# Three unread tiles of 32 bytes ahead of the coefficients, of split x and of the mixed heads, in a layer of float32 matmuls split in three

## The chip, the cores and the metric

The kernel runs on one core of a Trainium2 chip. The metric is the device time in microseconds of one execution. Before the change the median of three runs is 1747.68 us (1747.27 to 1749.12).

## What is computed

One decoder layer for 256 tokens of width 2048, in float32. Cut to what matters:

```python
h = x @ w_in + b_in                       # 2048 -> 5120 columns, in five parts
A = silu(layer_norm(causal_conv31(a_val * sigmoid(a_gate))))
Bm = sc_b * causal_conv3(sc_c * sc_h)
x1 = layer_norm(alpha * x + concat(A, Bm) @ w_out + b_out)
q = x1 @ w_q                              # 8 heads, two halves of 128
s = q . sub_keys                          # top 16 of 128, twice; top 16 of the 256 sums
experts, g = best 16 of 16384, softmax    # for every token and head
act = gelu(x1 . peer_u[experts])
f = sum over heads, k of act * g * peer_v[experts]
x2 = layer_norm(alpha * x1 + f)
```

## The kernel before

**Stages.** The kernel computes the experts densely. After the input projection (to about 235 us of the profile) comes the output projection (235 to 330), then the queries with the routing, then the products of x1 with all 16384 rows of peer_u (to about 1184), and the last projection from the 128 tiles of gated activations onto peer_v (1184 to 1735). Half of the last projection for the second block of 128 tokens is not done densely: for columns 0 to 1023 of that block POOL gathers, pick by pick, 128 rows from a copy of peer_v in DRAM (rows, row_late, line 582) and single coefficients (sp_coef, line 588), and DVE adds row times coefficient (line 1312).

**Split operands.** Every float32 product is made from three matmuls in fp32r: high by high, high by low, low by high. Weights stream from DRAM in units of 512 KB, which SP loads into raw (4 buffers) and, in the last projection, also into raw_late (3 more; RING is 7). ACT writes the high part w_hi (line 627), DVE the low part w_lo (line 843), each with SPLIT = 4 buffers; PE multiplies; each stage waits for the one ahead by semaphore, and SP loads a buffer again when DVE is done with it. ACT runs four units ahead of PE, DVE three.

**Which operand is stationary.** A matmul call names the output, the stationary operand, the moving operand. In the input projection, the queries and the products with peer_u the weights are stationary (128 columns) and split x (xt_hi, xt_lo, 256 columns) moves: lines 1411 to 1413. In the output projection mix_hi and mix_lo are stationary and the weights move, 512 columns: lines 1460 to 1462. In the last projection the coefficients (c_sets, made from hid on ACT line 776 and DVE line 1293) are stationary and the weights move, 512 columns: lines 1587 to 1589. For the last four units of the stream parts_of returns tail_hi and tail_lo in place of w_hi and w_lo. The gate matmuls (line 1553) have oh1 stationary and oh2g moving.

**Order of the last projection.** Four tiles are a group; each group has 8 units: column block 0, 2, 1, 3, two units each. Blocks 0 and 1 take one token block (6 matmuls a unit), blocks 2 and 3 both (12 a unit), 72 matmuls a group. The last four groups are run column block by column block. Coefficient sets c0 and c1 alternate in groups 0 to 28, the sets c2, c3 and c4 serve groups 29 to 31.

**Places in SBUF.** Tiles lie one after another, in the order in which they are named, each from a multiple of 32 bytes; an ExitStack that is closed gives its place back, so that later tiles lie over it. Bytes per partition: raw 16384 and w_hi, w_lo 8 x 4096, the first at a multiple of 64; stats 192, mv 16, rstd and neg_mean 8 each, so that what follows starts 288 bytes on. All tiles from c0 through acc, c2 to c4 and tail have sizes that are multiples of 64, except small ones inside the early set that no large matmul reads (prm, scpad: 32 and 8 bytes over together). hid, the early set, the routing tiles and c2 to c4 with tail lie over one another from the end of xt_lo on.

Of the kernel before, what the change touches and what calls it, by code (L numbers as in the profile page):

```python
# [5 lines left out]
P = 128  # L6
# [160 lines left out]
def build(nc, x_t, x_nat, w_in, w_out, w_q, u_w, v_w, params, sub_keys, b_out, ln1_g, ln1_b, ln2_g, ln2_b, out):  # L167
    f32 = mybir.dt.float32
# [10 lines left out]
    with ctx:  # L179
        def sb(name, shape, dt, where=ctx):  # L180
            return where.enter_context(nc.sbuf_tensor(name, shape, dt))
# [8 lines left out]
        mv = sb("mv", [P, TB, 2], f32)  # L190
        rstd = sb("rstd", [P, TB, 1], f32)
        neg_mean = sb("neg_mean", [P, TB, 1], f32)

        def coefs(name, where):
            return [sb(f"{name}_{part}", [P, GROUP, T], f32r, where) for part in ("hi", "lo")]
# [19 lines left out]
        raw_late = sb("raw_late", [P, RAW_LATE, HALF * P], f32, down1)  # L215
        rows = [sb(f"rows{i}", [P, JCOLS], f32, down1) for i in range(ROWS - 1)] + [row_late]
        down1.close()
        xt_hi = sb("xt_hi", [P, KT, T], f32r)
        xt_lo = sb("xt_lo", [P, KT, T], f32r)

        early = ExitStack()
        mix_hi = sb("mix_hi", [P, KT, T], f32r, early)
        mix_lo = sb("mix_lo", [P, KT, T], f32r, early)
# [1462 lines left out]
```

## Time and profile before

| what | value |
|---|---|
| median of three runs | 1747.68 us (1747.27 to 1749.12) |
| span of the profiled execution | 1745.8 us |
| PE, DVE, ACT, POOL busy | 1713.3, 1407.6, 854.0, 540.4 us |
| granted clock of PE, mean | 0.996 |
| moved by DMA | 504.5 MB, mean 289 GB/s |
| input projection, output projection | to 235 us, to 330 us |
| queries, routing, peer_u | to 1184 us |
| last projection | 1184 to 1735 us |

The span runs from the first to the last instruction of one profiled execution. Its own device time isn't given apart; the median of the runs lies 1.9 us above its span. PE is the tensor engine's matmuls, PEld its weight loads. A matmul's duration includes its way through the array, so that those of neighbours overlap: the distance between two starts says how fast they follow one another. The DMA share is the mean busy share of 16 engines; packets that overlap can bring it over 1.

### The profile page before, as it was taken

The page shows a single profiled execution, that of the slowest core. Times are in us where ns is not written, and L with a number is a line of the kernel's source. Part 1 is how long each engine was busy: PE and PEld are TensorE (multiplying, and loading weights), DVE is VectorE, ACT ScalarE, POOL GpSimd, SP SyncE. Part 2 cuts the span into 40 slices and gives each one's busy share as a digit, 9 for nine tenths or more (in the row PEclk, how much of TensorE's full clock was granted, in tenths as well). Part 3 has the DMA queues.
Part 4 walks back from the last instruction along what each step waited for, and adds up shares of the span by engine and source line. Part 5 has one row for each costly group of instructions (what it writes and reads, how often), then busy time and mean ns, then how long its engine had stood idle before and what let it go on. Part 6 is the DMA issues. An engine that isn't in the chain of part 4 may idle for free.

```text
span 1745.8 us, 31461 instructions
## 1 busy us (share of the span) xinstructions
PE 1713.3 (98%) x11910; PEld 1578.1 (90%) x11910; DVE 1407.6 (81%) x1998; ACT 854.0 (49%) x1084; POOL 540.4 (31%) x342
## 2 busy tenths in 40 slices
PE   8999999899999999999999999999999999999997
PEld 8999987799999999999999999998788777878776
DVE  7999997678967677777777777556899898999997
ACT  5544436344544444444444444445555555555544
POOL 0000000288881000000000000004787777777731
PEclk9999999999999999999999999999999999999999
DMA  7787787777777777777677777899899999999994
GB/s 267 267 276 267 234 260 249 273 237 235 250 249 252 238 236 244 247 235 239 237 241 239 236 244 243 282 355 332 314 400 400 399 401 389 400 399 395 369 398 133
DMA packets 173728, 504.52 MB, mean 289 GB/s; under 512 B 19408, under 2 KB 35920, under 8 KB 172624
## 3 DMA queue, kind: packets, MB, share of 16 engines
q1 hardware_dynamic: 134000, 427.08, 70.0%
q0 software_dynamic: 22528, 67.19, 10.0%
q10 hardware_dynamic: 17120, 9.35, 1.8%
q8 instruction: 29, 0.48, 0.1%
q14 instruction: 51, 0.42, 0.1%
HBM read 490.98 MB, written 79.69 MB: 327 GB/s over the span
## 4 chain that ended last, share of the span: by engine, by line
PE 78%; DMA 6%; DVE 6%; issue 5%; POOL 3%; ACT 1%; DVEq 1%; SPq 0%; POOLq 0%; ACTq 0%
PE psum L1411 18%; PE psum L1413 18%; PE psum L1412 18%; PE psum L1587 6%; PE psum L1589 6%; PE psum L1588 6%; POOL sp_coef L588 2%; DVE w_lo L843 2%; DMA raw<-in_v_w_dram 2%; PE psum L1553 2%; DMA raw_late<-in_v_w_dram 1%; PE psum L1460 1%; PE psum L1462 1%; PE psum L1461 1%; DVE psum L1312 1%
## 5 line engine op out<-in xcount | busy, mean ns | idle before, releaser
L627 ACT ACTIVATE w_hi<-raw 128x1024 fp32r<-128x1024 f32 x547 | 578.9, 1060 | 682.1 <-PE psum L1413 487.1
L1411 PE MATMUL psum<-xt_hi,w_hi 128*128 128x256 f32 x2944 | 827.2, 281 | 5.3 <-DVE xt_lo L857 3.1
L1412 PE MATMUL psum<-xt_lo,w_hi 128*128 128x256 f32 x2944 | 822.6, 279 | 0.0
L1413 PE MATMUL psum<-xt_hi,w_lo 128*128 128x256 f32 x2944 | 822.4, 279 | 0.0
L843 DVE TENSOR_TENSOR w_lo<-raw,w_hi 128x1024 fp32r<-128x1024 f32 x479 | 581.8, 1222 | 221.5 <-ACT w_hi L627 219.7
L1411 PEld LDWEIGHTS psum<-xt_hi,w_hi 128*128 128x128 f32 x2944 | 554.3, 188 | 6.6 <-issue 6.0
L1412 PEld LDWEIGHTS psum<-xt_lo,w_hi 128*128 128x128 f32 x2944 | 554.3, 188 | 0.0
L1413 PEld LDWEIGHTS psum<-xt_hi,w_lo 128*128 128x128 f32 x2944 | 554.1, 188 | 0.0
L582 POOL DMA_INDIRECT rows<-v_rows,sp_idx x96 | 130.9, 1364 | 709.7 <-issue 674.9
L1587 PE MATMUL psum<-w_hi,c_hi 128*128 128x512 f32 x752 | 299.7, 399 | 8.9 <-DVE w_lo L843 8.7
L1589 PE MATMUL psum<-w_hi,c_lo 128*128 128x512 f32 x752 | 298.2, 396 | 0.0
L1588 PE MATMUL psum<-w_lo,c_hi 128*128 128x512 f32 x752 | 297.9, 396 | 0.0
L571 POOL TENSOR_TENSOR w_lo<-raw,w_hi 128x1024 fp32r<-128x1024 f32 x68 | 164.7, 2427 | 364.3 <-ACT w_hi L627 364.2
L588 POOL DMA_INDIRECT sp_coef<-hid_spill,sp_idx x128 | 193.0, 1508 | 55.2 <-issue 45.9
L1587 PEld LDWEIGHTS psum<-w_hi,c_hi 128*128 128x128 f32 x752 | 141.7, 188 | 49.5 <-DVE w_lo L843 15.4
L1589 PEld LDWEIGHTS psum<-w_hi,c_lo 128*128 128x128 f32 x752 | 141.6, 188 | 34.3
L1588 PEld LDWEIGHTS psum<-w_lo,c_hi 128*128 128x128 f32 x752 | 141.7, 188 | 33.3
L627 ACT ACTIVATE w_hi<-raw_late 128x1024 fp32r<-128x1024 f32 x105 | 111.3, 1060 | 103.2 <-PE psum L1589 75.0
L843 DVE TENSOR_TENSOR w_lo<-raw_late,w_hi 128x1024 fp32r<-128x1024 f32 x105 | 126.6, 1221 | 8.4 <-ACT w_hi L627 8.4
L1312 DVE SCALAR_TENSOR_TENSOR psum<-rows,sp_coef,psum 128x1024 f32<-128x1024 f32 x95 | 121.8, 1282 | 3.2 <-DMA rows<-v_rows,sp_idx 2.3
L882 DVE SCALAR_TENSOR_TENSOR cacc<-apad,prm,cacc x232 | 101.3, 480 | 0.0
L1293 DVE TENSOR_TENSOR c_lo<-hid,c_hi 128x1024 fp32r<-128x1024 f32 x32 | 39.2, 1224 | 22.9 <-ACT c_hi L776 22.8
(164 smaller groups left out, 1131.8 us busy)
## 6 DMA issues: line engine op xcount, KB each, us to landing
raw<-in_u_w_dram SPq DMA_DIRECT2D x256, 512.0 KB, 4.2
raw<-in_v_w_dram SPq DMA_DIRECT2D x148, 512.0 KB, 8.7
v_rows<-in_v_w_dram SPq DMA_DIRECT2D x128, 512.0 KB, 5.2
raw_late<-in_v_w_dram SPq DMA_DIRECT2D x108, 512.0 KB, 8.9
raw<-in_w_in_dram SPq DMA_DIRECT2D x80, 512.0 KB, 4.3
raw<-in_w_out_dram SPq DMA_DIRECT2D x32, 512.0 KB, 4.5
raw<-in_w_q_dram SPq DMA_DIRECT2D x32, 512.0 KB, 4.5
hid_spill<-hid ACTq DMA_DIRECT2D x7, 1024.0 KB, 15.4
```

Source lines behind the costliest of these rows:

```text
L571: nc.gpsimd.tensor_tensor(w_lo[s][:, :], raw[:, s, :], w_hi[s][:, :].bitcast(f32), ALU.subtract).then_inc(lo_done[s], SPLIT)
L582: nc.gpsimd.indirect_dma_start(rows[k % ROWS][:, :], None, v_rows, bass.IndirectOffsetOnAxis(sp_idx[:, 1, k:k + 1], 0)).then_inc(rows_in[k ...
L588: nc.gpsimd.indirect_dma_start(sp_coef[:, k:k + 1], None, hid_dram, bass.IndirectOffsetOnAxis(sp_idx[:, 0, k:k + 1], 0)).then_inc(act_in[k ...
L627: nc.scalar.activation(parts_of(slot_u)[0][:, :], raw_of(slot_u), ACT.Copy).then_inc(hi_done, 1)
L843: tt(lo_w[:, :], raw_of(slot_u), hi_w[:, :].bitcast(f32), ALU.subtract).then_inc(lo_done[slot_u % SPLIT], SPLIT)
L1312: i = stt(picked[:, :], rows[k % ROWS][:, :], sp_coef[:, k:k + 1], picked[:, :], ALU.mult, ALU.add)
L1411: mm(dst, hi_w[:, sl], xt_hi[:, kk, :], start=st, stop=False)
L1412: mm(dst, hi_w[:, sl], xt_lo[:, kk, :], start=False, stop=False)
L1413: i = mm(dst, lo_w[:, sl], xt_hi[:, kk, :], start=False, stop=en)
L1587: mm(v_bank(j, b), c1, w1, start=st, stop=False)
L1588: mm(v_bank(j, b), c1, w2, start=False, stop=False)
L1589: i = mm(v_bank(j, b), c2, w1, start=False, stop=en)
```

## The change

Three tiles of 8 float32 (32 bytes a partition) that nothing reads or writes are named: one ahead of the coefficients, one ahead of split x, one ahead of what lies behind split x. No instruction is added, removed or moved. After it, modulo 64 bytes and counted from the split weights, c0, c1, the tiles that lie over them (gates, tables), raw_late and rows are at 0; split x is at 32, as before; mix, hid, the early and routing tiles, c2 to c4 and tail are at 0. Before, all of these were at 32.

```diff
@@ -190,6 +190,7 @@
         rstd = sb("rstd", [P, TB, 1], f32)
         neg_mean = sb("neg_mean", [P, TB, 1], f32)
+        sb("place_pad", [P, 8], f32)
 
         def coefs(name, where):
             return [sb(f"{name}_{part}", [P, GROUP, T], f32r, where) for part in ("hi", "lo")]
@@ -215,11 +216,13 @@
         rows = [sb(f"rows{i}", [P, JCOLS], f32, down1) for i in range(ROWS - 1)] + [row_late]
         down1.close()
+        sb("xt_pad", [P, 8], f32)
         xt_hi = sb("xt_hi", [P, KT, T], f32r)
         xt_lo = sb("xt_lo", [P, KT, T], f32r)
 
 
 
+        sb("early_pad", [P, 8], f32)
         early = ExitStack()
         mix_hi = sb("mix_hi", [P, KT, T], f32r, early)
         mix_lo = sb("mix_lo", [P, KT, T], f32r, early)
```

## Rows read from the trace of the kernel before

**Rows 1.** the page's part 1: engine, busy us, share of the span, instructions

```profile
...
PE 1713.3 (98%) x11910; PEld 1578.1 (90%) x11910; DVE 1407.6 (81%) x1998; ACT 854.0 (49%) x1084; POOL 540.4 (31%) x342
```

**Rows 2.** groups by form: line, operands, shapes, count, busy us, mean ns, idle before

```profile
...
L1411 PE MATMUL psum<-xt_hi,w_hi 128*128 128x256 f32 x2944 | 827.2, 281 | 5.3 <-DVE xt_lo L857 3.1 <-issue 2.3
...
L843 DVE TENSOR_TENSOR w_lo<-raw,w_hi 128x1024 fp32r<-128x1024 f32 x479 | 581.8, 1222 | 221.5 <-ACT w_hi L627 219.7
...
L1587 PE MATMUL psum<-w_hi,c_hi 128*128 128x512 f32 x752 | 299.7, 399 | 8.9 <-DVE w_lo L843 8.7
...
L843 DVE TENSOR_TENSOR w_lo<-raw_late,w_hi 128x1024 fp32r<-128x1024 f32 x105 | 126.6, 1221 | 8.4 <-ACT w_hi L627 8.4
...
L1460 PE MATMUL psum<-w_hi,mix_hi 128*128 128x512 f32 x128 | 51.0, 399 | 1.9 <-DVE mix_lo L997 1.1 <-DVE lnt L1024 0.8
...
L1553 PE MATMUL psum<-oh2g,oh 128*128 128x256 f16 x256 | 34.7, 277 | 0.0
...
L1587 PE MATMUL psum<-tail_hi,c_hi 128*128 128x512 f32 x16 | 6.2, 390 | 0.0
```

**Rows 3.** PE in order of time near the end: start us, us, line, operands

```profile
...
1718.97 0.40 PE L1587 MATMUL psum<-tail_hi,c_hi 128*128 128x512 f32 x1
...
1724.41 0.40 PE L1587 MATMUL psum<-w_hi,c_hi 128*128 128x512 f32 x1
...
1730.02 0.39 PE L1587 MATMUL psum<-tail_hi,c_hi 128*128 128x512 f32 x1
```

**Rows 4.** busy us (count) of PE, PEld, DVE, ACT, POOL; clock, DMA share, GB/s

```profile
...
1719.00:1724.40 5.40, 5.40 (x25) 4.48 (x24) 5.33 (x7) 0.95 (x1) 0.00 (x0) 1.00 0.00 0
1724.40:1730.00 5.60, 5.60 (x25) 4.51 (x24) 5.22 (x12) 2.50 (x6) 1.02 (x1) 1.00 0.00 0
```

**Rows 5.** PE in order of time, output projection

```profile
...
235.87 0.40 PE L1460 MATMUL psum<-w_hi,mix_hi 128*128 128x512 f32 x1
...
237.27 0.40 PE L1460 MATMUL psum<-w_hi,mix_hi 128*128 128x512 f32 x1
```

**Rows 6.** PE in order of time, a 256-column unit

```profile
...
899.78 0.28 PE L1412 MATMUL psum<-xt_lo,w_hi 128*128 128x256 f32 x1
...
900.71 0.28 PE L1411 MATMUL psum<-xt_hi,w_hi 128*128 128x256 f32 x1
```

**Rows 7.** PE in order of time, one batch of gate matmuls

```profile
...
594.35 1.08 PE L1553 MATMUL psum<-oh2g,oh 128*128 128x256 f16 x8
```

**Rows 8.** transfers of 1300 to 1700: GB/s in 40 slices; loads, median us to landing

```profile
...
GB/s 400 400 399 398 398 403 402 399 396 399 403 399 402 398 400 368 384 399 402 399 401 401 402 399 404 387 403 400 402 378 399 393 384 338 343 409 409 408 408 398
...
raw<-in_v_w_dram SPq DMA_DIRECT2D x105, 512.0 KB, 9.2
raw_late<-in_v_w_dram SPq DMA_DIRECT2D x81, 512.0 KB, 9.5
```

**Rows 9.** stretches, columns as in Rows 4

```profile
...
235.00:330.00 95.00, 92.63 (x403) 74.09 (x402) 74.85 (x94) 47.48 (x51) 4.07 (x2) 1.00 0.77 259
1184.00:1260.00 76.00, 74.85 (x319) 59.44 (x319) 56.82 (x51) 42.67 (x42) 47.45 (x37) 1.00 0.90 323
1260.00:1640.00 380.00, 374.42 (x1590) 298.60 (x1589) 356.79 (x317) 208.38 (x201) 293.28 (x202) 1.00 1.02 396
1500.00:1600.00 100.00, 99.46 (x426) 79.50 (x425) 96.62 (x86) 56.09 (x55) 77.04 (x54) 1.00 1.03 398
1640.00:1736.00 96.00, 93.50 (x398) 74.07 (x396) 83.19 (x86) 48.32 (x49) 30.72 (x23) 1.00 0.78 297
```

**Rows 10.** waits of 1260 to 1640: who for whom, us, times, longest

```profile
...
ACT w_hi L627 <- PE psum L1589: 121.7, 108, 2.2
...
ACT w_hi L627 <- DMA raw<-in_v_w_dram: 27.7, 27, 2.4
...
ACT w_hi L627 <- DMA raw_late<-in_v_w_dram: 21.2, 19, 1.8
```

## The prediction

> **What bounds the kernel now.** I read the busy shares first, then the two views that put a price on one matmul, then the one stage in which TensorE is not alone at its limit. PE is busy 98% of the span [rows 1]. So the end is set by how fast PE starts one matmul after another, and for that the duration column is of no use (281 and 399 ns, and they overlap); starts have to be subtracted. Three forms carry the span [rows 2]: 8832 matmuls of 256 columns (lines 1411 to 1413, x2944 each), 2256 + 48 of 512 columns in the last projection (lines 1587 to 1589, x752 and x16 each), and 384 of 512 columns in the output projection (lines 1460 to 1462, x128 each).
>
> Near the end the same three lines alternate between two kinds of operand within 11 us, on an idle DMA [rows 3, 4]. Units whose split weights lie in tail_hi/tail_lo: 24 starts from 1718.97 to 1724.41, 5.44 us, 226.7 ns apart. Units in w_hi/w_lo: 24 starts from 1724.41 to 1730.02, 5.61 us, 233.8 ns apart. The reader is to see that DVE (5.33 of 5.40 us and 5.22 of 5.60 us) is equally busy in both, that nothing is transferred in either, and that the clock is 1.00 in both [rows 4]. The slow spacing is the same 1500 us earlier under traffic: 235.87 to 237.27 us has 6 intervals, 233.3 ns [rows 5], in a stretch with a DMA share of 0.77 [rows 9]. So the 7 ns belong to the operands.
>
> **What distinguishes the operands.** Counting sizes modulo 64: w_hi and w_lo are at 0; stats to neg_mean take 288 bytes, so the coefficients, split x, mix and tail are all at 32. The last projection multiplies c (stationary, 32) by w (moving, 0), slow, or by tail (moving, 32), fast. The output projection is (32, 0), and slow [rows 5]. The 256-column units are (0, 32): 899.78 to 900.71, 8 intervals, 116.3 ns [rows 6], just half of 233. The gate matmuls are (32, 32), also 256 columns: eight of them end 1.08 us after the first starts [rows 7], and each takes 277 ns [rows 2], so seven intervals take 0.80 us, 115 ns: nearer to the fast rate's half (113.4) than to the slow one's (116.9), but no proof by itself. An absolute residue of the moving operand alone doesn't fit: the 256-column units have it at 32, as tail has, and run at the slow rate per column. Equal or unequal fits all. What no row shows is the pair (0, 0), which the change makes.
>
> **Part 1, place_pad:** coefficients c0 and c1 go to 0. **Part 3, early_pad:** mix, c2 to c4 and tail go to 0. **Part 2, xt_pad:** split x stays at 32 against w at 0, so the 8832 matmuls are left as they are: 0. The 48 tail matmuls stay an equal pair: 0. Gates, transposes and scores keep their pairs (both sides move by 32): 0. No instruction, wait or queue is added. Elementwise operands and DMA targets move too: raw against raw_late in the trace is exactly residue 0 against 32, and DVE takes 1222 against 1221 ns [rows 2], the landing 9.2 against 9.5 us [rows 8]; the last could be worth a per cent of the transfers' rate, or nothing; I take 0 and keep -1 to +3 us for it.
>
> **What PE alone would gain.** 2256 x 7.0 ns = 15.8 us in the last projection and 384 x 7.0 = 2.7 us in the output projection, 18.5 us. That is all, if nothing else is late: 1745.8 - 18.5 = 1727.3 us of span; the median of the runs lies 1.9 us above the profiled span, which I add: 1729.2.
>
> **What is late next.** In the output projection PE waited twice, 1.1 us for mix_lo and 0.8 us for the norm of the convolution [rows 2]. These chains don't get faster, so of the 1.3 us won ahead of the second half up to all can come back as wait: between 1.3 and 2.7 us, I take 2.0.
>
> The last projection is where it decides. From 1260 to 1640 us the DMA share is 1.02 at 396 GB/s [rows 9], in slices of 10 us mostly 398 to 403 [rows 8]; ACT waited 49 us of it for landings (27.7 + 21.2) and 122 us for PE [rows 10]; DVE is 93.9% busy (356.8 of 380). What arrives is the unit loads plus the row gathers, and both are paced by PE's units, so a PE that is 3% faster (7.0/233.8) asks for 3% more per us. PE already loses 5.6 us in these 380.
> - 1184 to 1260: DMA share 0.90 [rows 9], 74.9 us of PE x 3% = 2.2 us; DVE is busy 57 of 76 us, the transfers' last tenth is what is left, so I take 1.8.
> - 1260 to 1640: PE would like 374.4 x 3% = 11.2 us. The transfers can give only this: at the rate of the full slices, 400 GB/s, the same bytes (380 x 396) take 376.2 us, 3.8 us less; and the lead of the ring may be eaten up once. A load lands 9.2 to 9.5 us after its issue, one is issued every 2.15 us (105 + 81 in 400 us) [rows 8], so 4.3 of the 7 buffers are in flight and 2.7 are ahead, at most 5.8 us, of which PE can lose some 3.5 before it stops at the bursts. 3.8 + 3.5 = 7.3 us. DVE would need 93.9% / 0.975 = 96% of the time; for that and its queueing behind picks I take 0.4 off: 6.9.
> - 1640 to 1736: 93.5 x 3% = 2.8 us. The mean share there is 0.78 [rows 9], but the slices up to 1700 still read 398 to 409 GB/s [rows 8] and only what follows is free, so I take 1.8.
>
> Sum: 2.0 + 1.8 + 6.9 + 1.8 = 12.5 us. Span 1733.3, time 1735.2 us.
>
> **Rivals.**
> - *The transfers don't matter, PE takes all:* they are kept full only since buffers are free. For it: in 1500 to 1600 PE is 99.46% busy beside a share of 1.03 [rows 9]. Time 1729.2. The Trainium skill, page "DMA: Bandwidth & Descriptors", section "Where 436 GB/s comes from", gives a ceiling of 435 GB/s for the ports; by it 3% more than 400 would have room, and the time would be this one. No slice here goes over 409 [rows 8].
> - *The transfers hold everything while they are full:* the lead is worth nothing and the DVE queue eats the rest. Output 1.3 + early 1.8 + 3.8 less 1 us of DVE queueing + 1.0 at the end = 6.9 us: 1740.8.
> - *The period is 128 bytes, not 64:* by the sizes, c4 and tail, the fast pair, are equal modulo 128 as well, so the trace can't tell. Then c0 and c1 (64 off) gain nothing, and mix and c2 to c4 do: 2.0 us + three groups of 72 less the 48 tail ones, 168 x 7.0 ns = 1.2 us: 1744.5.
> - *No effect:* what makes tail fast is its place or that it is rewritten once, not its residue. Time 1747.7, and with tail's advantage lost 48 x 7 ns = 0.3 us more. Two pages of the Trainium skill speak for it: "TensorE: Matmul & The Clock Gate", in its walk through the matmul's steps, says that PE has two independent SBUF read ports, so that loading the next weights takes nothing from the running matmul; "SBUF — State Buffer", section "SBUF: two separate sides", that PE never waits on anyone. By either the relative place of the two operands could cost nothing; the starts of [rows 3] show 7 ns between two places, which neither explains.
> - *Slower:* the cost is of the two streams meeting in one half of a 64-byte line at offset 0 (only 32 with 32 is seen fast). If (0, 0) is as much worse than (32, 0) as (32, 32) is better, the 2256 + 384 matmuls cost 7.0 ns more each, 18.5 us, and the 48 of the tail 14 ns, 0.7 us: 1766.9. It ends above before as soon as (0, 0) is over 234 ns apart. Against it: nothing in [rows 3 to 7] depends on the sign of the difference: (0, 32) and (32, 0) cost the same per column.
>
> **How the numbers follow.** The forecast (equal pair fast, transfers take a third of it) 0.45; PE takes all 0.17; transfers hold it 0.18; period 128 0.06; no effect 0.09; slower 0.05. A measurement of this kernel can tell about 0.2%, 3.5 us, from no change: period 128, at -3.2, falls to "same" or just beside it, and I give it half to each. Faster 0.45 + 0.17 + 0.18 + 0.03 = 0.83, same 0.12, slower 0.05. The range goes from all for PE with the transfers' bonus down to 1728.5, and up to 1744.5, with period 128 at its edge; left out are no effect and slower, 0.14.
>
> **What would show it.** Starts of lines 1587 to 1589 and 1460 to 1462 some 226.7 ns apart where nothing waits, 116.3 ns still in the 256-column units; up to 235 us the trace unchanged to 0.5 us; the last projection begins 2 us earlier; from 1260 on a share of 1.03 with few lower stretches, ACT's wait for landings up from 49 us to 70 or more, PE's idle time in the last projection up from about 9 to 14 us. If starts stay at 233.8, the pair is not the cause; if only lines with c2 to c4 and mix speed up, the period is 128; if starts are fast and PE's idle time doesn't grow, the first rival holds.

## The result

The changed kernel takes 1776.6 us (median of 4 runs, 1774.7 to 1779.2) against 1747.5 us before in the same comparison: ratio 1.0162, 95% interval 1.0142 to 1.0181. It is 29 us slower where 12.5 us less was forecast; 1735.2 and the range of 1728.5 to 1744.5 are both missed, on the other side.

The page of the changed kernel, span and busy shares (columns as before):

```profile
span 1772.7 us, 31461 instructions
...
PE 1741.4 (98%) x11910; PEld 1605.7 (91%) x11910; DVE 1407.9 (79%) x1998; ACT 854.6 (48%) x1084; POOL 541.9 (31%) x342
```

PE is busy 98% of the span as before [rows 1], and 28 us longer in all. The groups of PE by form, to be laid beside [rows 2]: lines are three further down, the counts are the same, and the mean of the 256-column matmuls is 284 instead of 281 ns, that of the 512-column ones 397 instead of 399.

```profile
...
L1414 PE MATMUL psum<-xt_hi,w_hi 128*128 128x256 f32 x2944 | 835.3, 284 | 4.2 <-DVE xt_lo L860 2.3 <-issue 1.9
...
L1590 PE MATMUL psum<-w_hi,c_hi 128*128 128x512 f32 x752 | 298.9, 397 | 8.9 <-DVE w_lo L846 8.5
...
L1463 PE MATMUL psum<-w_hi,mix_hi 128*128 128x512 f32 x128 | 50.9, 398 | 1.9 <-DVE mix_lo L1000 1.0 <-DVE lnt L1027 0.9
```

PE in order of time in a 256-column unit (start us, us, line, operands), for [rows 6], and in the last projection:

```profile
...
899.80 0.28 PE L1415 MATMUL psum<-xt_lo,w_hi 128*128 128x256 f32 x1
...
900.76 0.29 PE L1414 MATMUL psum<-xt_hi,w_hi 128*128 128x256 f32 x1
```

```profile
...
1599.81 0.39 PE L1590 MATMUL psum<-w_hi,c_hi 128*128 128x512 f32 x1
...
1601.68 0.39 PE L1592 MATMUL psum<-w_hi,c_lo 128*128 128x512 f32 x1
```

Eight intervals take 0.96 us, 120.0 ns, where [rows 6] have 116.3. In the last projection eight intervals take 1.87 us, 233.8 ns: nothing won. The stretches, to be laid beside [rows 9] (busy us and count of PE, PEld, DVE, ACT, POOL; granted clock, DMA share, GB/s), the last three 28 us later than there:

```profile
...
600.00:1000.00 400.00, 400.00 (x3344) 396.22 (x3343) 284.14 (x375) 183.24 (x308) 0.00 (x0) 1.00 0.72 233
1212.00:1288.00 76.00, 74.22 (x317) 58.94 (x316) 55.95 (x50) 42.33 (x42) 47.57 (x36) 1.00 0.89 321
1288.00:1668.00 380.00, 375.06 (x1598) 298.82 (x1597) 358.19 (x318) 209.35 (x203) 296.11 (x202) 1.00 1.02 397
1668.00:1764.00 96.00, 92.32 (x394) 73.17 (x392) 83.89 (x87) 47.96 (x49) 30.59 (x23) 1.00 0.78 293
```

From 600 to 1000 us PE is never idle and does 3344 matmuls; before it did 3433 in the same 400 us (shown below, beside x_up_64). DMA share, rate and DVE's share in the last projection are those of before.

Taken apart by the starts of the first and the last matmul of each stage: input projection 231.9 us (before 225.7), output projection 92.5 (92.7), queries to peer_u 878.0 (856.0), last projection 550.2 (551.4). The input projection and the third stage are the two with 256-column matmuls. Together they take 28.2 us more, a little over the 26.9 by which the whole span grew. 8832 matmuls at 119.97 instead of 116.66 ns (means of all distances under 140 ns between starts of these lines) are 29.2 us.

### The profile page after: what moved, and what is told of

Its sections match the earlier page's. It is cut to its first block, busy times and chain, and to the rows that moved or that the text cites. A ratio compares the mean times of both kernels' runs of the same rounds, so it can differ in the third digit from the quotient of the medians.

```text
span 1772.7 us, 31461 instructions
## 1 busy us (share of the span) xinstructions
PE 1741.4 (98%) x11910; PEld 1605.7 (91%) x11910; DVE 1407.9 (79%) x1998; ACT 854.6 (48%) x1084; POOL 541.9 (31%) x342
## 4 chain that ended last, share of the span: by engine, by line
PE 84%; DMA 5%; DVE 4%; issue 3%; POOL 1%; ACT 1%; DVEq 0%; SPq 0%; POOLq 0%; ACTq 0%
PE psum L1416 20%; PE psum L1415 20%; PE psum L1414 20%; PE psum L1590 6%; PE psum L1592 6%; PE psum L1591 6%; DVE w_lo L846 2%; DMA raw_late<-in_v_w_dram 2%; PE psum L1556 2%; DMA raw<-in_v_w_dram 1%; PE psum L1463 1%; PE psum L1465 1%; PE psum L1464 1%; DVE psum L1315 1%; DMA rows<-v_rows,sp_idx 1%
## 5 line engine op out<-in xcount | busy, mean ns | idle before, releaser
L1416 PE MATMUL psum<-xt_hi,w_lo 128*128 128x256 f32 x2944 | 832.9, 283 | 0.0
L585 POOL DMA_INDIRECT rows<-v_rows,sp_idx x96 | 142.6, 1485 | 723.9 <-issue 691.6
L591 POOL DMA_INDIRECT sp_coef<-hid_spill,sp_idx x128 | 183.1, 1430 | 55.6 <-issue 46.4
L1590 PEld LDWEIGHTS psum<-w_hi,c_hi 128*128 128x128 f32 x752 | 141.2, 188 | 49.9 <-DVE w_lo L846 15.8
```

Of the source, the lines that this page charges most:

```text
L585: nc.gpsimd.indirect_dma_start(rows[k % ROWS][:, :], None, v_rows, bass.IndirectOffsetOnAxis(sp_idx[:, 1, k:k + 1], 0)).then_inc(rows_in[k ...
L591: nc.gpsimd.indirect_dma_start(sp_coef[:, k:k + 1], None, hid_dram, bass.IndirectOffsetOnAxis(sp_idx[:, 0, k:k + 1], 0)).then_inc(act_in[k ...
L1416: i = mm(dst, lo_w[:, sl], xt_hi[:, kk, :], start=False, stop=en)
L1590: mm(v_bank(j, b), c1, w1, start=st, stop=False)
```

## The experiments

Distances here are those from the start of the stationary operand to the start of the moving one, modulo 256 where nothing else is said. By the sizes (raw starts 1152 bytes into a partition): split x lies 46368 bytes behind w_hi0 in the kernel before, that is 32 modulo 256 (288 modulo 1024), and 96 (352) in the changed one. Weights less coefficients is 224 before; in the changed kernel 192 for c0 and c1, and 128 for mix and c2 to c4. The spacings in the tables are means over the starts in the trace of each run.

**Which tile does it.** Four kernels, one pad each:

```diff
# x_up_64 (x_up_32 and x_up_128 with [P, 8] and [P, 32])
+        sb("xt_pad", [P, 16], f32)
         xt_hi = sb("xt_hi", [P, KT, T], f32r)
# all_up_64
+        sb("first_pad", [P, 16], f32)
         raw = sb("raw", [P, RAW, HALF * P], f32)
```

> One unread tile of 64 bytes ahead of split x and nothing else: split x lies exactly where the changed kernel has it (63968 against 63904 bytes), while c0, c1, raw_late and rows stay where the kernel before has them. If the place of split x against the split weights is what made the 256-column matmuls slower (theory X), their starts are 119.9 to 120.0 ns apart, as after, and the time is 1747.5 + 29 = 1776 us. If it was another tile that moved (theory O: coefficients, gate tiles or raw_late, as operands or as neighbours), the starts stay at 116.7 ns and the time at 1747 us. If only residues modulo 64 count, as I had predicted, also 116.7 ns.

> 32 bytes ahead of split x: equal to the split weights modulo 64, 64 off modulo 128. By the residue modulo 64 with equal pairs fast (my recorded theory) the 256-column starts are 113.4 ns apart: 8832 x 3.3 ns less, 1718 us. By a distance with a period of 128 or more (theory X) it is a new point, between 113 and 120 ns. By theory O 116.7 ns, 1747 us.

> 128 bytes ahead of split x. If what counts has a period of 128 bytes, the 256-column starts are again 116.7 ns apart and the time is 1747 us. If the period is 256 or longer, or it is no period at all, they differ from 116.7 ns by over 0.5 ns.

> 64 bytes ahead of raw, the first tile: every tile lies 64 bytes further, all distances between tiles are as before. If distances between operands count, nothing changes: 116.7 and 233.3 ns, 1747 us. If the absolute place of split x counts (it is again at 63968, as in the changed kernel), the 256-column starts are 120 ns apart and the time is 1776 us.

Measured: x_up_64 1779.1 us, ratio 1.0169 (1.0147 to 1.0191), 119.97 ns; x_up_32 1755.9 us in one run, 117.8 ns; x_up_128 1764.6 us in one run, 118.4 ns; all_up_64 1747.1 us in one run, 116.7 ns. The stretch of 600 to 1000 us, in the order before, x_up_64, all_up_64, where the count of PE is what tells the pace:

```profile
...
600.00:1000.00 400.00, 400.00 (x3433) 396.51 (x3433) 293.00 (x385) 187.34 (x314) 0.00 (x0) 1.00 0.72 239
```

```profile
...
600.00:1000.00 400.00, 400.00 (x3345) 396.29 (x3344) 284.47 (x374) 183.01 (x309) 0.00 (x0) 1.00 0.72 234
```

```profile
...
600.00:1000.00 400.00, 400.00 (x3434) 396.50 (x3433) 292.59 (x384) 187.70 (x316) 0.00 (x0) 1.00 0.75 239
```

Moving split x by the 64 bytes by which the change moves it gives the whole loss. Moving everything by 64 bytes gives nothing, though split x then lies where the changed kernel has it: not a place counts but a distance. The pad ahead of split x also moves what lies behind it (mix, hid, the routing tiles, c2 to c4, tail); c0, c1, raw_late and rows stay where they were, so they have no part in the loss. That it is split x and none of the tiles behind it is shown by all_aligned and x_64_rest_0 further down: they differ, modulo 1024, in the place of split x alone, and their starts are 119.9 and 117.8 ns apart. x_up_32, equal modulo 64, is slower than before and not faster: the residue modulo 64 is not the measure.

**Distances as a whole.** In all_aligned the four small tiles are named last instead of ahead of the coefficients, so that all distances are 0 modulo 1024. In the two runs with steps the four buffers lie 32 bytes apart from each other:

```diff
# all_aligned
-        stats = sb("stats", ...)   # and mv, rstd, neg_mean: moved behind sp_tok
# steps_0_to_96, also
-        w_hi = [sb(f"w_hi{i}", ...) for i in range(SPLIT)]
-        w_lo = [sb(f"w_lo{i}", ...) for i in range(SPLIT)]
+        for i in range(SPLIT):
+            if i:
+                sb(f"slot_pad{i}", [P, 8], f32)
+            w_hi.append(sb(f"w_hi{i}", ...))
+            w_lo.append(sb(f"w_lo{i}", ...))
# steps_128_to_224, also
+        sb("behind_pad", [P, 32], f32)
```

> The 288 bytes of stats, mv, rstd and neg_mean are named last, behind sp_tok, instead of ahead of the coefficients; nothing is added. Every distance between two operands of a large matmul is then a multiple of 1024 bytes, as tail against c4 is in the kernel before (its starts are 226.7 ns apart). Theory X1 (distance 0 is the fast one in every form): 256-column starts 113.4 ns apart, 512-column 226.7 ns; PE alone would gain 8832 x 3.3 + 2640 x 7.0 = 47.6 us, of it the transfers hold back up to 11 in the last projection: 1700 to 1712 us. Theory X2 (distance matters, but 0 is good only where the weights move against coefficients, and other distances are best in the other form): 512-column starts 226.7, 256-column ones at 116.7 to 120 ns. Theory X3 (what made tail fast is not its distance): 512-column starts stay at 233.3 ns and the time is 1747 us or above.

> As all_aligned, but the four buffers of the split weights lie 0, 32, 64 and 96 bytes further (high and low part alike), so that one run holds four distances in each form: split x less weights 96, 64, 32, 0 bytes in buffers 0 to 3 (the last modulo 1024), weights less coefficients and less mix the negatives of these. The time says little; the starts inside a unit, sorted by buffer, are what is read. By the single distances seen so far for the 256-column form (32: 116.7, 64: 117.8, 96: 120.0 ns, measured modulo 256): buffer 2 at 116.7, buffer 1 at 117.8, buffer 0 at 120.0 if the period is 256 or a divisor; if it is longer, other numbers. Buffer 3 by X1 at 113.4 and 226.7 ns.

> As steps_0_to_96, with 128 bytes more behind the split weights: split x less weights 224, 192, 160, 128 bytes in buffers 0 to 3, weights less coefficients the negatives. For 160 the run with 128 bytes ahead of split x showed 118.4 ns: buffer 2 repeats it if the period is 256. If the period is 128, buffers 0 to 3 repeat 96, 64, 32, 0 of the other run.

Measured: all_aligned 1772.4 us, ratio 1.0142 (1.0121 to 1.0164), 256-column starts 119.9 ns apart, 512-column ones 227.2 in the last and 227.0 in the output projection. PE in order of time in its last projection, seven intervals in 1.59 us:

```profile
...
1599.86 0.39 PE L1589 MATMUL psum<-w_hi,c_lo 128*128 128x512 f32 x1
...
1601.45 0.39 PE L1587 MATMUL psum<-w_hi,c_hi 128*128 128x512 f32 x1
```

So tail was fast by its distance, and 0 is the fast distance with 512 moving columns and a bad one with 256 (X2). The runs with steps, one execution each (1766.8 and 1759.9 us), sorted by buffer, for the 256-column form:

| distance of x from weights | 0 | 32 | 64 | 96 | 128 | 160 | 192 | 224 |
|---|---|---|---|---|---|---|---|---|
| ns, stepped buffers | 119.8 | 117.0 | 114.7 | 120.0 | 118.8 | 119.6 | 114.4 | 118.4 |
| ns, all buffers alike | 119.9 | 116.7 | 117.8 | 120.0 | | 118.4 | see below | |

32, 96 and 0 repeat what kernels with all buffers alike showed. 64 does not (114.7 against 117.8 in x_up_32), and 160 does not either (119.6 against 118.4 in x_up_128), which the expectation had put as the sign of a period of 256. Here a mean hides two values: at its one distance x_up_128 ran at 117.3 ns in the queries and the first units of peer_u (340 to 522 us) and at 118.7 ns before and after. So a distance can have more than one spacing, and what the neighbouring buffers do counts; that asked for the next runs.

**Fast distances for both forms, and what holds the last projection.**

```diff
# x_64_rest_0: all_aligned, and (x_192_rest_0: 192 bytes, and 832)
+        sb("xt_pad", [P, 16], f32)
         xt_hi = sb("xt_hi", [P, KT, T], f32r)
...
+        sb("mix_pad", [P, 240], f32, early)     # brings mix back to 0
+        sb("late_pad", [P, 240], f32, down2)    # c2 to c4 and tail too
# aligned_less_dve: all_aligned, and
-    i = stt(picked[:, :], rows[k % ROWS][:, :], sp_coef[:, k:k + 1], picked[:, :], ...)
+    i = stt(picked[:, 0:DCH // 2], rows[k % ROWS][:, 0:DCH // 2], sp_coef[:, k:k + 1], picked[:, 0:DCH // 2], ...)
# aligned_less_dma: all_aligned, and for n % 2 and n >= 24
-    sp.dma_start(raw_of(u), src)
+    sp.dma_start(raw_of(u)[:, 0:3 * DCH // 2], src[:, 0:3 * DCH // 2])
```

> As all_aligned, with split x 64 bytes behind the split weights (modulo 1024) in all units; mix and all coefficient sets stay at 0. Theory P256 (the pattern repeats after 256 bytes): split x at 64 is the same as the 320 of the run with 32 bytes ahead of split x, so 117.8 ns between 256-column starts, 119.9 to 117.8 against all_aligned, 1772 - 19 = 1753 us. Theory P-long (it does not repeat before 512 bytes): buffer 1 of steps_0_to_96 was at 64 and showed 114.65, so 114.7 ns; 8832 x 5.2 = 46 us less than all_aligned, 1726 us, which would be 21 us under the kernel before.

> The same with split x 192 bytes behind. In steps_128_to_224 the buffer at 192 showed 114.4 ns. Theory P-long: 114.4 ns, 1724 us, as good as 64 or better. If a buffer's neighbours in the other run made it fast (theory N: what the three other buffers do counts), both this and x_64_rest_0 come out between 116 and 120 ns, 1740 us or above.

> all_aligned, with each of the 127 later picks added over 256 of its 1024 columns only (the other 768 columns of the second token block's first half get the first pick alone); every transfer is left as it is. all_aligned has 512-column starts 6.3 ns closer than before, 14.2 us, but its last projection takes 549.3 against 551.4 us: PE's stalls there, clock drops among them, rose from 14 to 26 us. Theory T (the transfers' rate holds it): stalls stay over 20 us, the stage at 547 us or more. Theory V (DVE, 94% busy, holds it): stalls fall to 5 us or less, the stage takes 527 to 532 us.

> all_aligned, with every second unit load of the last projection, from the 25th on, cut to three quarters of its columns (the rest of the buffer holds an older unit); DVE, ACT and PE do all they did. The unit loads ask for an eighth less, 31 of 400 GB/s. Theory T: stalls fall to 5 us or less and the stage takes 527 to 532 us. Theory V: stalls stay over 20 us. If both this and aligned_less_dve fall half way, each is late on its own, and their sum decides.

Measured: x_64_rest_0 1757.6 us, ratio 1.0045 (1.0028 to 1.0061), 117.8 ns; x_192_rest_0 1754.1 us, ratio 1.0020 (1.0009 to 1.0030). 114 ns, which the stepped run had shown, came in neither but for one stage. Theory P256 holds: 64 with all buffers alike is as slow as the 320 of x_up_32, so these two are one distance, and 256 is a multiple of the period. In x_192_rest_0 the same operands at the same distance had two spacings, in order of time:

```profile
...
149.75 0.28 PE L1415 MATMUL psum<-xt_lo,w_hi 128*128 128x256 f32 x1
...
150.66 0.28 PE L1414 MATMUL psum<-xt_hi,w_hi 128*128 128x256 f32 x1
```

```profile
...
699.75 0.28 PE L1415 MATMUL psum<-xt_lo,w_hi 128*128 128x256 f32 x1
...
700.69 0.28 PE L1414 MATMUL psum<-xt_hi,w_hi 128*128 128x256 f32 x1
```

Eight intervals in 0.91 us (113.8; the mean up to 230 us is 113.3 with single distances of 113 and 114), then in 0.94 us (117.5; mean 117.8), and no unit lies between, but for the first few of either stretch. So at 192, and by the stepped run at 64, there are two rhythms, and either holds for hundreds of matmuls. The fast one did not shorten this execution: its input projection took 221.5 us where x_192_again (below, the same program) took 227.6, but its output projection took 94.0 instead of 90.7, with 3.1 instead of 1.3 us of waiting for mix_lo and 3.4 us at half the granted clock, and its last projection 555.1 instead of 549.2.

aligned_less_dve leaves out three quarters of the columns that DVE adds for the later picks; aligned_less_dma leaves out a quarter of every second load, an eighth of these bytes. The last projection, by first and last start: all_aligned 549.3 us, aligned_less_dve 547.9 us, aligned_less_dma 542.9 us, against 551.4 before. PE's time above its pace in it (all distances over 260 ns, less 233 ns each) is 14.4 us before, 25.7 in all_aligned, 24.1 less DVE, 19.7 less DMA. The middle of it in all_aligned, aligned_less_dve and aligned_less_dma (columns as above):

```profile
...
1290.00:1670.00 380.00, 368.55 (x1589) 296.67 (x1587) 354.77 (x315) 210.08 (x203) 287.93 (x204) 1.00 1.02 395
```

```profile
...
1290.00:1670.00 380.00, 370.89 (x1602) 299.20 (x1601) 282.55 (x320) 210.79 (x203) 251.25 (x208) 1.00 1.03 399
```

```profile
...
1290.00:1670.00 380.00, 373.41 (x1626) 304.49 (x1625) 362.86 (x324) 212.76 (x206) 308.32 (x207) 1.00 1.00 371
```

all_aligned does 1589 matmuls in 380 us, before 1590 [rows 9], though its starts are 6 ns closer. With 72 of 355 us of DVE's work taken away the share of DMA stays at 1.03 and ACT's wait for landings rises, from 63.5 to 143.1 us; PE does 1602:

```profile
...
ACT w_hi L627 <- DMA raw<-in_v_w_dram: 85.7, 80, 3.3
...
ACT w_hi L627 <- DMA raw_late<-in_v_w_dram: 57.4, 58, 2.7
```

With transfers taken away ACT no longer waits for one in that stretch and PE does 1626, at DVE 95% busy. Less work for DVE gives 1.4 us and leaves 24.1 us of stalls, as theory T had it. Less to transfer gives 6.4 us, not the 17 to 22 that theory T had put (527 to 532 us), and 19.7 us of stalls, just under what V had put. So the transfers bind first. That DVE binds next is argued from its 95% and from PE's waits there, which are all for w_lo; no run relieves both.

**The forecast's own case, and a way to the fast rhythm.**

```diff
# x_32_rest_0: as x_64_rest_0 with 32 bytes ahead of split x (992 ahead of mix and of c2)
# buffers_64_192: x_64_rest_0, and
-        w_hi = [...]; w_lo = [...]
+        for i in (0, 2, 1, 3):
+            if i == 1:
+                sb("slot_pad", [P, 32], f32)
+            w_hi[i] = sb(f"w_hi{i}", ...)
+            w_lo[i] = sb(f"w_lo{i}", ...)
# parts_192_64: x_64_rest_0, and
         w_hi = [...]
+        sb("part_pad", [P, 32], f32)
         w_lo = [...]
```

> As x_64_rest_0 with split x 32 bytes behind the split weights (modulo 1024) and all stationary coefficients and mix at 0: my forecast's own case, the 256-column units left at the pace of before and every 512-column matmul at 226.7 ns. Before has split x at 288 modulo 1024. If the pattern has a period of 256 (theory P256), 288 and 32 are the same and the starts are 116.7 ns apart; if not, another number. With 116.7 ns, the output projection 2.0 us shorter (as in all_aligned) and the last projection between 549 and 553 us, as in all_aligned and x_64_rest_0 (transfers hold it), the time is 1744 to 1748 us. By the sum of my prediction it would be 1735.

> The same program as x_192_rest_0, whose profile had 113.3 ns between 256-column starts up to 230 us and 117.8 ns from 335 us on, at one and the same distance. Theory M (at 192 and 64 bytes two rhythms hold themselves, and which one is caught is set by how the stream starts after a pause): the profile of this other execution shows 113.3 in some stages and 117.8 in others, not in the same ones as before, or the same ones if the start is alike; no value between. If the spacing were a function of distance and stage alone, it repeats 113.3 and 117.8 in the same places.

> Split x 192 bytes behind the split weights in buffers 0 and 2, 64 bytes behind them in buffers 1 and 3 (weights less coefficients -128 and 0). Theory M: in steps_0_to_96 and steps_128_to_224 the buffers at 64 and 192, entered from a buffer at another distance, showed 113.5 to 114.9 ns; if a change of distance at each unit lets the stream catch the fast rhythm, these are 113.3 to 115 ns here too, and the time is 1747 - 8832 x 2 to 3 ns, 1722 to 1730 us, plus at most 3 for the last projection. If the rhythm, once 117.8, holds over a change of 128 bytes, all stay at 117.8: 1757 us.

> Split x 192 bytes behind the high part and 64 bytes behind the low part of the weights, so that the distance changes twice in each group of three matmuls. Theory M with a change that lets the fast rhythm be caught: 113.3 to 115 ns, 1722 to 1730 us. If the slow rhythm holds over the change: 117.8 ns, 1757 us. If a change itself costs: over 117.8 ns.

Measured: x_32_rest_0 1747.6 us over 12 runs (1740.8 to 1750.5), ratio 0.9983 (0.9970 to 0.9997), 116.7 and 227.2 ns, output projection 90.7 us, last projection 551.7 us. x_192_again 1754.2 us, 117.8 ns in every stage: the rhythm of the input projection was another one in this execution of the same program. buffers_64_192 1723.3 us, ratio 0.9855 (0.9831 to 0.9878), 113.4 ns in the input projection and 114.4 later; parts_192_64 1721.3 us, ratio 0.9841 (0.9817 to 0.9864), 113.4 and 113.5 ns. The stretch of 600 to 1000 us of x_64_rest_0, x_192_again and parts_192_64:

```profile
...
600.00:1000.00 400.00, 400.00 (x3401) 396.44 (x3400) 290.66 (x382) 185.65 (x312) 0.00 (x0) 1.00 0.69 237
```

```profile
...
600.00:1000.00 400.00, 400.00 (x3401) 396.44 (x3400) 290.89 (x382) 185.64 (x312) 0.00 (x0) 1.00 0.74 237
```

```profile
...
600.00:1000.00 400.00, 400.00 (x3521) 396.52 (x3521) 300.74 (x395) 192.82 (x325) 0.00 (x0) 1.00 0.76 245
```

3521 matmuls in 400 us against 3401, and 3433 before. A distance that alternates between 64 and 192 by part held spacings of 113 to 115 ns in nearly every unit of the two profiles taken (parts_192_64, and parts_and_256 below). By buffer the fast rhythm was lost in the queries, where nearly all units ran at 117.8 ns, and in one unit in six of peer_u beside the gates. PE in order of time in the queries of buffers_64_192, 12 intervals in 1.41 us, 117.5 ns:

```profile
...
389.76 0.28 PE L1419 MATMUL psum<-xt_lo,w_hi 128*128 128x256 f32 x1
...
391.17 0.28 PE L1419 MATMUL psum<-xt_lo,w_hi 128*128 128x256 f32 x1
```

A distance that stays at either of the two caught the fast rhythm in one of eight stages seen (the input projection and what follows, in x_up_32, x_64_rest_0, x_192_rest_0 and x_192_again). Why a stream falls into it, and what the rhythm is of, the records do not show: in the two stretches of x_192_rest_0 most weight loads start 2 to 5 ns after a matmul in both; they take 187 or 188 ns in the fast one, and in the slow one a third of them 192.

**Where tiles begin that are loaded.** In these two kernels the last projection took only 542.0 and 543.2 us, with 512-column starts 230.5 and 228.9 ns apart, and the rate of the transfers was higher. Their raw_late and rows begin at multiples of 256 bytes of a partition; in all kernels ahead of them at 96, 128, 160, 192 or 224 beyond one.

```diff
# x_32_from_256: x_32_rest_0, and
+        sb("first_pad", [P, 32], f32)
         raw = sb("raw", [P, RAW, HALF * P], f32)
# parts_and_256: parts_192_64 with raw named behind w_lo
```

> x_32_rest_0 with 128 unread bytes ahead of raw, the first tile. All distances between operands stay, so PE's starts stay (116.7 and 227.1 ns). raw, raw_late and the rows now begin at multiples of 256 bytes of a partition (raw began at 1152, 128 beyond one). Theory W (transfers into tiles that begin at multiples of 256 bytes go faster): as in buffers_64_192 and parts_192_64, whose rows and raw_late lay at such multiples, the full slices of the last projection read 412 to 415 GB/s instead of 400 to 403, and the stage gets shorter, 535 to 542 us instead of 551.7, so 1731 to 1738 us. Theory S (those two kernels moved more because their PE stage came at another pace, 229 to 230.5 ns): 400 to 403 GB/s, 1747 us.

> parts_192_64 with raw behind the split weights instead of ahead of them: distances as there (192 and 64 bytes, weights less coefficients -128 and 0), and raw too at a multiple of 256 bytes, not only raw_late and the rows. By theory W the four sevenths of the unit loads that go to raw get faster too: another 1 to 3% of rate in the full slices and 1 to 5 us less in the last projection than the 543.2 of parts_192_64, 1716 to 1720 us. By theory S 1721 us, and 1721 too if only the rows matter.

Measured: x_32_from_256 1739.0 us, ratio 0.9922 (0.9901 to 0.9944), 116.7 and 227.1 ns, last projection 544.7 us; parts_and_256 1717.4 us over 5 runs, ratio 0.9793 (0.9771 to 0.9815), last projection 549.6 us in its profile. The transfers of 360 us of the last projection, x_32_rest_0 and then x_32_from_256, from 80 us after its start (GB/s in 40 slices; loads, median us from issue to landing):

```profile
...
GB/s 398 390 375 403 382 394 360 401 402 398 400 402 399 400 403 399 398 403 401 398 399 390 383 384 393 398 401 402 398 403 398 381 383 379 402 400 401 404 387 398
...
raw<-in_v_w_dram SPq DMA_DIRECT2D x96, 512.0 KB, 8.9
raw_late<-in_v_w_dram SPq DMA_DIRECT2D x71, 512.0 KB, 9.1
```

```profile
...
GB/s 378 401 398 416 343 382 331 418 415 416 416 419 417 416 419 400 395 418 417 415 417 418 418 416 418 417 416 416 418 418 407 375 383 418 418 391 376 378 402 356
...
raw<-in_v_w_dram SPq DMA_DIRECT2D x98, 512.0 KB, 7.5
raw_late<-in_v_w_dram SPq DMA_DIRECT2D x73, 512.0 KB, 7.5
```

Full slices go from 398 to 404 up to 415 to 419 GB/s, and a load lands after 7.5 instead of 8.9 us, with every distance between operands kept. Theory W holds for the rate; the stage, 544.7 us, stayed 3 us above what it had put. The Trainium skill, page "DMA: Bandwidth & Descriptors", section "How a descriptor splits into AXI transactions", says of the transactions that read that they must start at a multiple of 256 bytes, so that a descriptor that starts elsewhere pays for the bytes from the boundary below it. It does not say so of the place that is written, which is what moved here. These rows agree in direction, with 4% for packets of 4096 bytes. By an estimate from that page, a packet that starts 128 bytes beyond a boundary takes 17 transactions in place of 16, 6% more, or 132 pieces of 32 bytes in place of 128, 3% more. raw seems to count beside raw_late and rows: with the latter two at multiples (parts_192_64) the full slices read mostly 409 to 415 and a load into raw landed after 8.7 us, with all three (parts_and_256) they read 415 to 420, and the load took 7.5. But the last projection of parts_and_256 took 6.4 us longer than that of parts_192_64 and not less, as was expected, in one execution each; the cause is open.

## Why the prediction was wrong

**The measure was wrong (What distinguishes the operands).** That the 7 ns belong to the operands was right, and all_aligned showed that they come from the distance: 227 ns at 0 in both 512-column stages. The failed step is "Equal or unequal fits all", counted modulo 64. The facts under it were tail at 0 (fast), the other 512-column matmuls at 224 and the 256-column ones at 32 (slow), and the gates at 0 (called no proof). They fit any period of 64 or more. I named 128 as a rival and stopped there. The period is 256: 64 and 320 bytes both give 117.8 ns and 32 and 288 both 116.7, while 32 and 160, 128 apart, differ.

**Part 2 was costed at nothing (xt_pad).** "Split x stays at 32 against w at 0, so the 8832 matmuls are left as they are: 0" is the step that turned the sign. It stays at 32 modulo 64, but goes from 32 to 96 modulo 256, and that costs 8832 x 3.3 = 29 us: x_up_64 has the whole loss alone. It was the term with by far the largest count, and it deserved bounds from both sides, since of distances other than 0 only 32 and 224 had been seen.

**Parts 1 and 3 bring nothing to PE.** 15.8 and 2.7 us were forecast; c0 and c1 land at 192, mix and c2 to c4 at 128, and the starts stay at 233.2 and 232.9 ns. So -18.5 us by PE alone became -0.3. The rival of a period of 128 had mix and c2 to c4 faster; they are not.

**The term for the last projection was too large even with the spacing given.** x_32_rest_0 is the case that the forecast meant. Its output projection is 2.0 us shorter, as put; its last projection 551.7 us against 551.4, where 10.5 us less was forecast. In all it came out 1.9 us under the kernel before of the same comparison (1749.5), where the forecast had 12.5 and the rival that the transfers hold everything 6.9. That rival had the mechanism, but its price for the last projection, 5.6 us, was too high as well: neither the lead of the ring (3.5 us of the forecast) nor the slices not quite full (3.8 us of both) were to be had. PE's waits in that stage rose from 8.7 to 17.8 us. In its middle the rate was 395 GB/s with slices down to 360, not fuller than before, and the granted clock was at half for 6.8 us and again for 3.4 us, against 3.4 us before. That each longer stall of PE also holds up the loads that wait for its buffers would explain it, but no run tests that.

**The targets of transfers were read modulo 64 too (the term of -1 to +3 us).** "Exactly residue 0 against 32" compared raw with raw_late, which lie 128 and 160 bytes beyond a multiple of 256, and the change took raw_late to 192. None of these is at a multiple; with raw, raw_late and rows at multiples the last projection is 7 us shorter (x_32_from_256 against x_32_rest_0).

**The rivals of the other side.** "Slower" was put as (0, 0) modulo 64 being bad for 512 columns, 1766.9. The change made that pair in all 512-column matmuls but those of tail's units, and the starts stayed at 233 ns; in all_aligned, where it is also 0 modulo 256, they are 227 ns apart. So the 0.05 given to "slower" met the sign by another cause, the distance of split x, which that rival left alone. "No effect" is refuted as a cause of tail's speed by all_aligned. The rules cited from the Trainium skill ("TensorE: Matmul & The Clock Gate" on two independent read ports, "SBUF — State Buffer", section "SBUF: two separate sides", on PE never waiting) leave no room for these runs: at six distances of split x, with the same instructions, starts lie 113 to 120 ns apart. Whether PE's two reads are what disturb each other, no run shows.

**What the signs said.** "116.3 ns still in the 256-column units" failed at 120.0; "some 226.7 in lines 1587 to 1589" failed at 233.1 in the mean. Up to 235 us the trace was not unchanged to 0.5 us but 6.2 us longer. These were the right things to look at. One sign would have misled: "if starts stay at 233.8, the pair is not the cause" came true, though the distance of the pair is the cause, with another period.

## What to carry to other kernels

When two operands' places seem to set a pace, take the distance between them with a period no shorter than the rows exclude, and write down for each large group which distance it has before and after; a pad ahead of one tile moves all behind it. Price first the group with the largest count, even if the change means to leave it alone. Measure distances on the chip: one kernel with a different offset in each buffer of a ring gives a table from one execution, but check what it says with all buffers alike, since at some distances the spacing changed with what ran beside it (160: 119.6 and 118.4 ns).

## What the runs showed that was not expected

- The spacing of fp32r matmuls depends on the distance between stationary and moving operand, period 256 bytes: with 256 moving columns 116.7 ns at 32, 117.8 at 64, 117.3 or 118.7 at 160, 119.9 at 0, 120.0 at 96; with 512 columns 227 at 0, 229 at 64 (one buffer of the stepped runs) and 232.6 to 234.6 at all other multiples of 32. It is not the distance of the one pair alone: in parts_192_64, with the high parts at 128 and the low ones at 0, all 512-column starts lie 228.9 ns apart.
- At 64 and 192 bytes there is a second rhythm of 113.3 ns; a distance that alternates between the two within each group of three matmuls held it or came within 2 ns: 3521 matmuls in 400 us for 3433.
- 4096-byte packets into tiles that begin at multiples of 256 bytes of a partition: 415 to 419 GB/s in full slices against 398 to 404.
- Both together, with nothing but unread bytes and the order of names, give 1717.4 us for 1751.9, ratio 0.9793 (0.9771 to 0.9815): the fastest version seen.
